# A hybrid pooling/SSM/MoE block on one core: second half of the down matrices behind experts three and four, last round by tiles, u read back ahead of the output projection

## The chip, the cores and the metric

The kernel runs on one core of a Trainium2 chip. The metric is the device time of one execution in microseconds. The profile is one more execution, taken by the hardware profiler; its times below count from the first instruction.

## The reference

One layer over 256 latent tokens of width 1024, with a prefix of 256 context tokens, float32 throughout:

```python
mod = silu(c) @ w_mod + b_mod              # shift, scale and gate, twice
h   = rmsnorm(x, g_mix) * (1 + sc1) + sh1  # the same for the context
u   = h @ w_in                             # 512 columns pooled, 512 for the SSM
pool = pool_mixer(u[:, :512])              # centred means, four windows
ssm  = glu(gelu(scan_fwd(u_ssm) + scan_bwd(u_ssm) + d * u_ssm))
x   = x + g1 * (concat(pool, ssm) @ w_out)
h2  = rmsnorm(x, g_ffn) * (1 + sc2) + sh2
eidx, gate = route(h2)                     # best of 4 groups, top 2 of its 8 experts
y   = moe(h2)                              # 32 experts: (silu(x@Wg) * (x@Wu)) @ Wd, hidden width 512
out = rmsnorm(x + g2 * y, g_final)
```

The scans start from the final state of the context's scan.

## The kernel before

Each engine has a program of its own and the engines meet at semaphores (`wait_ge`, `then_inc`). SP issues nearly all loads, in one hand-written order: its queue is in order, so a wait in SP's program holds back every load behind it. ScalarE and GpSimd issue a few transfers of their own.

**The mixer.** The modulation's first two thirds are products on TensorE, of `w_mod` in eight row chunks each (`mod_chunk`, semaphore `mod_used`). The last third is loaded in eight pieces of 1 MiB (`last_third(j, gate)`, four with gate 0 for the scale, four with gate 1 for the gate) and summed on VectorE by `mod_sum` (lines 1405 and 1408, semaphore `mod2_used`). GpSimd's `mod_bias` adds the bias row to each, and `modulation(gate)` on TensorE sums over the partitions.

For the SSM, u is computed in four parts (`u_ssm`), taken from PSUM by ScalarE into `ut`, written to the DRAM tensor `u_scratch` in two halves (line 1041, `u_out0`, `u_out1`) and read back in another layout by eight reads each (line 308, `u8_in0`, `u8_in1`). `state_inputs(h)` on TensorE (line 655) makes the inputs of the scans from each half, ScalarE takes them out (`take_states`), and VectorE runs the scan of each half, then fills `HP` (`hp_ready`). Before the second half's reads SP issues `wo_ssm`, the lower half of `w_out`, 2 MiB. Behind ScalarE's `take_states(0)` stand two copies of the lag kernels (`KT`), which TensorE waits for, and 15 transfers that build a Toeplitz table (`toeplitz`, `toep_in`), which both TensorE and the writing of `HP` wait for.

Then come GELU (ScalarE), the GLU product (line 759), VectorE's products into `cat` (`cat_ssm`, line 1204), the product with `w_out` (`mix_pool`, line 711, for the pooled half and line 799 for the SSM half), the residual, the second norm, and the router. `modulation(1)` (line 748) stands ahead of the counting product (`counts`, lines 823 and 824), and the one-hot gather (line 835) takes rows of each expert's tokens into `xm`.

**The experts.** They go by in rounds of four, `four(i)`, i from 0 to 7. `wts` has two buffers for the gate and up matrices of one expert each (4 MiB), and there are four places for down matrices (2 MiB each). A round moves 24 loads of 1 MiB: 8 for experts one and two, 8 for three and four, 8 for the down matrices. SP's functions for them are `next_two(i - 1)` (experts one and two of round i), `second_two(i)` (experts three and four) and `downs(i, half)` (half of each down matrix). `second_two(i)` waits for `gu_half`, which TensorE raises after each half of an expert; each of its four waits stands in front of two loads. `downs(i, 0)` waits until round i - 1 has used its first halves (`down_half`), `downs(i, 1)` until that round's `down` has ended (`down_mm`). In the last round the second halves go as two quarters each (`down_load_one`).

TensorE's round is: `gate_up(i, 0)` to `gate_up(i, 3)` (lines 863 and 864), transposes of the hidden rows (line 879), the scatter of the round before (line 841), `down(i)` (line 903, 128 instructions) and the gathers for the next round (line 835). A matmul of a float32 operand appears as two instructions.

**The end.** In the last round `down` goes over n = 2h + t (column half h, token tile t) in the order 0, 1, 2, 3. VectorE scales each n by the gate (`four_out`). TensorE scatters both tiles' first column halves, then both second ones. ScalarE squares and sums each tile, GpSimd makes (mean + eps) ** -0.5 of the sum, VectorE multiplies each half tile by that and by `g_final` in one instruction (line 1589), and SP and ScalarE store.

SP's order in the inner rounds and in the last one is:

```python
with sp.Fori(1, last_four) as i:
    downs(i, 0)
    downs(i, 1)
    second_two(i)
    next_two(i)
downs(last_four, 0)
second_two(last_four)
```

Of the kernel before, what the change touches and what calls it, by code (L numbers as in the profile page):

```python
# [7 lines left out]
ALU = mybir.AluOpType  # L8
# [50 lines left out]
def hybrid_block(nc, x, ctx, w_mod, columns, ssm_bc, b_mod_rows, w_in, w_out, w_pool, w_glu, w_router, b_router,  # L59
# [9 lines left out]
    FC = F // P  # L69
    NC = T // L  # L70
    DG = 32
    GP = 16

    with ExitStack() as stack:
# [183 lines left out]

        def store(eng, t, h):

            eng.dma_start(out[0, t * P:(t + 1) * P, 512 * h:512 * (h + 1)],
                          xn2[:, t, 512 * h:512 * (h + 1)]).then_inc(S("out_done"), 16)

        @block.sync
        def _(sp):
# [36 lines left out]
            for h in range(2):  # L302
                if h == 1:
                    sp.wait_ge(S("u_ssm_mm"), 4)
                    sp.dma_start(wo_ssm, w_out_v[:, 4:8, :]).then_inc(S("wo_ssm_in"), 16)
                sp.wait_ge(S(f"u_out{h}"), 16)
                for s in range(L):
                    sp.dma_start(ra[SG * s:SG * (s + 1), 0:2048].rearrange("i (g n) -> i g n", g=8)[:, :, 128 * h:128 * h + 128],
                                 u_dram.rearrange("(g i) (w s n) -> w s i g n", g=8, w=2, s=L)[h, s]).then_inc(S(f"u8_in{h}"), 16)
# [6 lines left out]

            sp.wait_ge(S("mod_used"), 14)
# [88 lines left out]
        def _(gp):  # L406
            gp.memset(cb[:, 2048:4096], 0.0).then_inc(S("cb_zero"), 1)

            gp.wait_ge(S("mhalf_set"), 1)
# [64 lines left out]
            def mod_bias(gate):  # L474

                gp.wait_ge(S("mod2_used"), KD * gate + KD)
                for n in range(2):
                    j = 2 * gate + n
# [8 lines left out]
            for t in range(2 * NT):  # L487
                if t == NT:

                    gp.dma_start(gfb, g_final.rearrange("(a d) -> a d", a=1).broadcast_to([P, D])).then_inc(S("gf_in"), 16)  # L490
                gp.wait_ge(S("ss2_ready" if t < NT else "ss3_ready"), t % NT + 1)
# [3 lines left out]
                if t == NT - 1:  # L495
# [4 lines left out]
                    gp.memset(PT, 0.0).then_inc(S("zeroed"), 1)  # L500

        @block.tensor
        def _(pe):
# [238 lines left out]
            def modulation(gate):  # L743

                pe.wait_ge(S("mod2_sum"), 2 * gate + 2)
                for h in range(2):
                    j = 2 * gate + h
                    mm = pe.matmul(ps[:, 6 + h, :], ones, acc[:, 512 * j:512 * j + 512], start=True, stop=True)
                return mm

            modulation(0).then_inc(S("scale_mm"), 1)
# [66 lines left out]
            modulation(1).then_inc(S("gate_mm"), 1)  # L818
# [8 lines left out]
            BANKS = (6, 7, 4, 5)  # L827
            GATHER = (6, 7, 5, 6)
# [9 lines left out]
            def scatter(h, stop=False):  # L838

                for t in range(NT):  # L840
                    mm = pe.matmul(ps[:, 2 * t + h, :], PT[:, t, :], oS[:, 2 * h + t, :], start=False, stop=stop, skip_group_check=True)  # L841
                return mm
# [47 lines left out]
            def down(i, last):  # L890

                pe.wait_ge(S("hid_ready"), 4 * i + 4)
                for f in range(FC):
# [4 lines left out]
                    for n in range(4):  # L898
# [739 lines left out]
```

## Time and profile before

| | |
|---|---|
| median of 3 runs | 661.68 us (659.23 to 661.77) |
| the profiled execution | 661.11 us |
| its span, first to last instruction | 659.3 us |
| mean granted clock of TensorE | 0.965 |
| TensorE busy | 588.4 us (89%) |
| VectorE busy | 196.1 us (30%) |
| ScalarE busy | 132.0 us (20%) |
| moved by DMA | 249.02 MB, mean 378 GB/s |

### The profile page before, as it was taken

What the parts mean: (1) busy time and instruction counts of PE and PEld (TensorE: products, weight loads), DVE (VectorE), ACT (ScalarE), POOL (GpSimd) and SP (SyncE); (2) the same over time, 40 slices, a digit from 0 to 9 for tenths busy, and PEclk for the clock granted to TensorE, in tenths of its full rate; (3) what the DMA queues carried; (4) which work ended last, traced back from release to release, by engine and by line L of the source; (5) the groups of instructions that cost most, each with busy time, mean ns of one, the idle gap of its engine ahead of it and who ended that gap; (6) DMA issues with size and microseconds to landing.
All of it is one profiled execution on the core that took longest, in us unless ns stands there. A gap on an engine that the chain in (4) does not pass through costs nothing.

```text
span 659.3 us, 9355 instructions
## 1 busy us (share of the span) xinstructions
PE 588.4 (89%) x3770; PEld 249.9 (38%) x3770; DVE 196.1 (30%) x426; ACT 132.0 (20%) x226; POOL 53.3 (8%) x103
## 2 busy tenths in 40 slices
PE   1999968889899997899799879979997997899995
PEld 0454544455553342234233323423342342234331
DVE  7998458988730020002001000200100010002003
ACT  8661312031213111012020201111021102012111
POOL 3894000012010000000000000000000000000000
PEclk9999979999979999999799989989998999999999
DMA  8993999998779999999999999999999999999951
GB/s 330 418 402 110 319 327 292 401 410 351 299 281 409 422 419 421 422 417 422 422 421 420 423 421 421 420 421 422 422 422 422 423 421 421 421 421 375 403 227 64
DMA packets 43609, 249.02 MB, mean 378 GB/s; under 512 B 4776, under 2 KB 7480, under 8 KB 17216
## 3 DMA queue, kind: packets, MB, share of 16 engines
q1 hardware_dynamic: 41240, 243.93, 91.2%
q10 hardware_dynamic: 1992, 3.68, 1.7%
q0 software_dynamic: 352, 1.07, 0.5%
q8 instruction: 17, 0.28, 0.2%
q14 instruction: 8, 0.07, 0.0%
HBM read 244.46 MB, written 2.11 MB: 374 GB/s over the span
## 4 chain that ended last, share of the span: by engine, by line
PE 56%; DMA 21%; DVE 2%; issue 1%; SPq 0%; ACT 0%; POOL 0%; DVEq 0%
PE ps L863 21%; DMA wts<-in_w_up 21%; PE ps L903 17%; PE ps L835 5%; PE ps L841 5%; PE ps L799 2%; PE ps L711 1%; PE ps L879 1%; PE ps L759 1%; PE ps L727 1%; SPq L243 0%; PE ps L864 0%; DVE rc L1204 0%; DVE ra L1589 0%; PE ps L791 0%
## 5 line engine op out<-in xcount | busy, mean ns | idle before, releaser
L863 PE MATMUL ps<-wts,ra 128*64 128x512 f32 x512 | 242.5, 626 | 34.2 <-DMA wts<-in_w_up 33.0
L864 PE MATMUL ps<-wts,ra 128*64 128x512 f32 x512 | 242.6, 626 | 0.0
L863 PEld LDWEIGHTS ps<-wts,ra 128*64 128x64 f32 x512 | 70.0, 143 | 180.3 <-issue 133.5
L903 PE MATMUL ps<-wts,ra 128*32 128x512 f32 x512 | 111.4, 593 | 0.0
L903 PE MATMUL ps<-rc,ra 128*32 128x512 f32 x512 | 111.4, 593 | 0.0
L1204 DVE TENSOR_TENSOR ra<-ra,ps 128x256 f32<-128x256 f32 x32 | 13.5, 422 | 268.7 <-ACT ra L1150 268.6
L1144 ACT COPY ra<-ps 128x512 f32<-128x512 f32 x32 | 33.6, 1050 | 218.6 <-PE ps L864 218.6
L864 PEld LDWEIGHTS ps<-wts,ra 128*64 128x64 f32 x512 | 70.0, 143 | 0.0
L903 PEld LDWEIGHTS ps<-wts,ra 128*32 128x32 f32 x512 | 29.1, 110 | 73.2 <-issue 73.2
L1204 DVE TENSOR_TENSOR cb<-ps,ra 128x512 f32<-128x512 f32 x32 | 22.1, 692 | 103.4 <-PE ps L903 103.4
L1139 ACT COPY ra<-ps 128x512 f32<-128x512 f32 x32 | 18.8, 586 | 148.4 <-PE ps L835 148.4
L492 POOL TENSOR_SCALAR small<-small 128x1 f32<-128x1 f32 x4 | 0.8, 188 | 475.6 <-ACT ra L1185 467.7
L835 PEld LDWEIGHTS ps<-cb,ra 128*128 128x128 f32 x256 | 31.4, 200 | 13.6 <-issue 8.6
L835 PE MATMUL ps<-cb,ra 128*128 128x128 f32 x256 | 34.5, 291 | 1.1 <-issue 1.1
L841 PE MATMUL ps<-cb 128*128 128x512 f32 x68 | 32.9, 606 | 0.0
L622 PE MATMUL ps<-ra,wts 128*128 128x512 f32 x64 | 29.6, 600 | 0.6 <-ACT ra L1025 0.6
L903 PEld LDWEIGHTS ps<-rc,ra 128*32 128x32 f32 x512 | 29.2, 110 | 0.0
L1204 DVE TENSOR_TENSOR cb<-cst,ut 128x256 f32<-128x256 f32 x16 | 6.7, 421 | 47.9 <-PE ps L835 46.6
L879 PEld LDWEIGHTS ps<-cst,ra 128*128 128x128 f32 x128 | 14.2, 141 | 17.2 <-issue 15.3
L520 PE MATMUL ps<-wts,sil 128*32 128x512 f32 x96 | 13.4, 649 | 7.4 <-DMA wts<-in_w_mod 7.2
L879 PE MATMUL ps<-cst,ra 128*128 128x128 f32 x128 | 18.8, 280 | 0.0
L841 PEld LDWEIGHTS ps<-cb 128*128 128x128 f32 x68 | 11.6, 190 | 15.5 <-issue 14.6
(226 smaller groups left out, 509.4 us busy)
## 6 DMA issues: line engine op xcount, KB each, us to landing
wts<-in_w_up SPq DMA_DIRECT2D x64, 1024.0 KB, 15.5
wts<-in_w_gate SPq DMA_DIRECT2D x64, 1024.0 KB, 13.4
wts<-in_w_down SPq DMA_DIRECT2D x30, 1024.0 KB, 8.6
rc<-in_w_down SPq DMA_DIRECT2D x30, 1024.0 KB, 12.4
wts<-in_w_mod SPq DMA_DIRECT2D x16, 1024.0 KB, 13.4
r<-in_w_mod SPq DMA_DIRECT2D x6, 1024.0 KB, 10.9
wts<-in_w_out SPq DMA_DIRECT2D x2, 2048.0 KB, 11.5
wts<-in_w_in SPq DMA_DIRECT2D x2, 1024.0 KB, 19.8
```

The costliest lines, as they stand in the source:

```text
L520: mm = pe.matmul(ps[32 * j:32 * j + 32, bank, :], silc[:, k, :], w[:, 512 * j:512 * j + 512], start=False, stop=(k == KD - 1))
L622: mm = pe.matmul(ps[:, 4 + q % 2, :], WBs[:, k, P * q:P * q + P], hT[:, k, :], start=(k == 0), stop=(k == KD - 1))
L799: mm = pe.matmul(ps[:, n, :], cat[:, 4 + k, P * (n // 2):P * (n // 2) + P], wo_ssm[:, k, 512 * (n % 2):512 * (n % 2) + 512], start=False, ...
L835: mm = pe.matmul(o, h2P[:, t, k, :], Pm[:, t], start=True, stop=True, skip_group_check=True)
L841: mm = pe.matmul(ps[:, 2 * t + h, :], PT[:, t, :], oS[:, 2 * h + t, :], start=False, stop=stop, skip_group_check=True)
L863: pe.matmul(ps[0:64, 4 + b, :], st, Wg[b][:, k, :], start=(k == 0), stop=(k == KD - 1))
L864: mm = pe.matmul(ps[64:128, 4 + b, :], st, Wu[b][:, k, :], start=(k == 0), stop=(k == KD - 1))
L879: mm = pe.transpose(ps[:, 6 + j % 2, P * f:P * f + P], gu[:, j % 2, P * f:P * f + P], ident)
L903: mm = pe.matmul(ps[32 * j:32 * j + 32, BANKS[n], :], hid[:, j, f, SLOTS * t:SLOTS * t + SLOTS], Wd[j][:, f, 512 * h:512 * h + 512], start ...
L1139: act.copy(xm[:, 2 * r:2 * r + 2], ps[:, GATHER[r], :].rearrange("p (k e s) -> p k e s", k=2, e=4)).then_inc(S("xm_ready"), 1)
L1144: act.copy(gu[:, j % 2, :].rearrange("p (f q) -> p q f", f=FC), ps[:, 4 + j % 2, :].rearrange("p (q f) -> p q f", f=FC)).then_inc(S("gu_co ...
L1204: return dve.tensor_tensor(o, a, b, op)
```

## The change

- **u.** The eight reads of the second half go out as soon as its write has landed, four from SP and four from ScalarE (behind `take_states(0)`), and the load of `wo_ssm` moves behind them and behind modulation chunks 6 and 7.
- **The gate's bias.** GpSimd adds the bias row only for the scale. For the gate, TensorE adds it in `gate_product`, with a product of one row for each half.
- **The order of the expert loads.** Round one is written out in the old order. From round two on `second_two(i)` stands between the two halves of `downs`. In the last round `second_two` comes ahead of `downs(last_four, 0)`.
- **The last round.** n goes 0, 2, 1, 3, so both halves of tile 0 come first. VectorE multiplies by sqrt(D) and `g_final` without waiting for the norm's factor, and the factor (of the sum, not the mean) is applied afterwards in place, to three half tiles on ScalarE and one on VectorE. The stores are spread anew.
- Two pairs of semaphores become one each (`consts_set`, and `ss2_ready` for `ss3_ready`).

```diff
+        def u8_load(eng, h, lags):
+            for s in lags:
+                eng.dma_start(ra[SG * s:SG * (s + 1), 0:2048]..., u_dram...[h, s]).then_inc(S(f"u8_in{h}"), 16)
...
             for h in range(2):
-                if h == 1:
-                    sp.wait_ge(S("u_ssm_mm"), 4)
-                    sp.dma_start(wo_ssm, w_out_v[:, 4:8, :]).then_inc(S("wo_ssm_in"), 16)
                 sp.wait_ge(S(f"u_out{h}"), 16)
-                for s in range(L):
-                    sp.dma_start(ra[SG * s:SG * (s + 1), 0:2048]..., u_dram...[h, s]).then_inc(S(f"u8_in{h}"), 16)
+                u8_load(sp, h, range(L // 2 if h else L))
                 for k in range(3 + 3 * h, min(6 + 3 * h, KD)):
                     mod_chunk(1, k)
...
+            sp.wait_ge(S("u_ssm_mm"), 4)
+            sp.dma_start(wo_ssm, w_out_v[:, 4:8, :]).then_inc(S("wo_ssm_in"), 16)
             sp.wait_ge(S("mod_used"), 14)
...
             second_two(0)
             next_two(0)
+            downs(1, 0)
+            downs(1, 1)
+            second_two(1)
+            next_two(1)
...
-            with sp.Fori(1, last_four) as i:
+            with sp.Fori(2, last_four) as i:
                 downs(i, 0)
+                second_two(i)
                 downs(i, 1)
-                second_two(i)
                 next_two(i)
+            second_two(last_four)
             downs(last_four, 0)
-            second_two(last_four)
...
-            for t in range(NT):
-                sp.wait_ge(S("fin_ready"), 2 * t + 1)
-                store(sp, t, 0)
+            for h in range(2):
+                sp.wait_ge(S("fin_act"), h + 1)
+                store(sp, 0, h)
+            sp.wait_ge(S("fin_ready"), 1)
+            store(sp, 1, 1)
...
# GpSimd
-            mod_bias(0)
-            mod_bias(1)
+            mod_bias()
+            gp.wait_ge(S("mod2_used"), 2 * KD)
...
+            for t in range(NT):
+                gp.wait_ge(S("ss2_ready"), NT + t + 1)
+                gp.tensor_scalar(ms2[:, 2 + t:3 + t], ms2[:, 2 + t:3 + t], float(D * EPS), None, ALU.add)...
+                gp.tensor_tensor(rstd2[:, 2 + t:3 + t], ms2[:, 2 + t:3 + t], mhalf, ALU.pow)...
...
# TensorE
+            def gate_product():
+                pe.wait_ge(S("mod2_used"), 2 * KD)
+                for h in range(2):
+                    j = 2 + h
+                    pe.matmul(ps[:, 6 + h, :], ones[32 * j:32 * j + 1, :], modrow[32 * j:32 * j + 1, 2, :], start=True, stop=False)
+                    mm = pe.matmul(ps[:, 6 + h, :], ones, acc[:, 512 * j:512 * j + 512], start=False, stop=True)
...
-            modulation(1).then_inc(S("gate_mm"), 1)
+            gate_product().then_inc(S("gate_mm"), 1)
...
+            TILE_ORDER = (0, 2, 1, 3)
...
-                    for n in range(4):
+                    for n in (TILE_ORDER if last else range(4)):
...
-            pe.wait_ge(S("out_copy"), 4 * last_four + 6)
             pe.wait_ge(S("pt_copy"), last_four + 2)
-            scatter(0, True)
-            pe.wait_ge(S("out_copy"), 4 * last_four + 8)
-            for t in range(NT):
-                pe.matmul(ps[:, 2 * t + 1, :], PT[:, t, :], oS[:, 2 + t, :], start=False, stop=True,
+            for at, n in enumerate(TILE_ORDER):
+                h, t = n // 2, n % 2
+                pe.wait_ge(S("out_copy"), 4 * last_four + 5 + at)
+                pe.matmul(ps[:, 2 * t + h, :], PT[:, t, :], oS[:, n, :], start=False, stop=True,
                           skip_group_check=True).then_inc(S("y_ready"), 1)
...
# ScalarE
             take_states(0)
+            act.wait_ge(S("u_out1"), 16)
+            u8_load(act, 1, range(L // 2, L))
...
-                act.wait_ge(S("y_ready"), t + 1)
+                act.wait_ge(S("y_ready"), 2 * t + 2)
...
+            for at, (t, h) in enumerate(((0, 0), (0, 1), (1, 0))):
+                act.wait_ge(S("rstd2_ready"), NT + t + 1)
+                act.wait_ge(S("gf_scaled"), at + 1)
+                v = xn2[:, t, 512 * h:512 * h + 512]
+                act.mul(v, v, rstd2[:, 2 + t:3 + t]).then_inc(S("fin_act"), 1)
+            act.wait_ge(S("fin_act"), 3)
+            store(act, 1, 0)
...
# VectorE
-            four_out(last_four)
+            four_out(last_four, (0, 2, 1, 3))
...
             for t in range(NT):
-                dve.wait_ge(S("rstd2_ready"), 3 + t)
+                dve.wait_ge(S("ss2_ready"), NT + t + 1)
                 for h in range(2):
                     c0 = slice(512 * h, 512 * h + 512)
-                    dve.scalar_tensor_tensor(xn2[:, t, c0], ps[:, 2 * t + h, :], rstd2[:, 2 + t:3 + t], gfb[:, c0],
-                                             ALU.mult, ALU.mult).then_inc(S("fin_ready"), 1)
+                    dve.scalar_tensor_tensor(xn2[:, t, c0], ps[:, 2 * t + h, :], ROOT_D, gfb[:, c0],
+                                             ALU.mult, ALU.mult).then_inc(S("gf_scaled"), 1)
+            dve.wait_ge(S("rstd2_ready"), 2 * NT)
+            dve.wait_ge(S("gf_scaled"), 2 * NT)
+            v = xn2[:, 1, 512:1024]
+            dve.tensor_scalar(v, v, rstd2[:, 3:4], None, ALU.mult).then_inc(S("fin_ready"), 1)
```

## Rows read from the trace of the kernel before

**Rows 1.** Stretches by round, six and seven; columns as in the first line.

```profile
core 0: us, PE busy (x) PEld busy (x) DVE busy (x) ACT busy (x) POOL busy (x), PEclk, DMA share, GB/s
537.23:596.85 59.62, 53.70 (x316) 20.36 (x315) 5.54 (x11) 8.10 (x13) 0.00 (x0) 0.97 1.01 422
596.85:649.07 52.22, 52.03 (x316) 19.91 (x315) 5.21 (x10) 8.14 (x13) 0.00 (x0) 1.00 0.73 289
```

**Rows 2.** The chain that ended last, rounds six and seven: start, us, what.

```profile
574.60 0.64 PE ps L863
...
596.85 1.98 PE ps L835 x16
...
626.82 0.64 PE ps L863
...
635.20 13.87 PE ps L903 x128
```

**Rows 3.** Timeline around the bounce of u; the last line is line 1041's landings.

```profile
76.44 0.33 ACTq L1041 DMA_DIRECT2D u_scratch<-ut  x1
...
85.52 3.89 SPq L308 DMA_DIRECT2D ra<-u_scratch  x8
...
92.29 6.67 PE L655 MATMUL ps<-ra,wts 128*64 128x64 f32 x128 [5.32 <-DMA ra<-u_scratch]
...
DMA to landing us min/median/max: 3.3/6.2/9.1
```

**Rows 4.** Timeline of VectorE, the start of the second scan.

```profile
100.14 1.36 DVE L1204 TENSOR_TENSOR cb<-wts,cb 128x256 f32<-128x256 f32 x3 [7.43 <-ACT wts L1054]
```

**Rows 5.** Stretches of the mixer, columns as in rows 1.

```profile
76.00:104.00 28.00, 22.68 (x316) 14.82 (x312) 15.22 (x50) 9.42 (x16) 0.00 (x0) 0.88 0.85 296
104.00:152.00 48.00, 41.37 (x440) 24.73 (x435) 42.78 (x102) 10.88 (x20) 2.51 (x2) 1.00 1.02 385
```

**Rows 6.** The gate's first third: issue, landing; its use, cat_ssm, w_out's product (timeline, chain).

```profile
131.25 0.38 SPq L295 DMA_DIRECT2D wts<-in_w_mod  x1
...
wts<-in_w_mod SPq DMA_DIRECT2D x1, 1024.0 KB, 10.2
...
143.63 0.75 DVE L1405 TENSOR_SCALAR cb<-wts,sil 128x1024 f32<-128x1024 f32 x1
...
151.18 2.03 DVE L1204 TENSOR_TENSOR wts<-rc 128x256 f32<-128x256 f32 x4
...
153.21 3.43 PE ps L799 x8
```

**Rows 7.** Timeline of TensorE from the counts to the first gate_up.

```profile
179.93 0.41 PE L823 MATMUL ps<-cb,cst 128*128 128x64 f32 x2 [1.89 <-DVE cb L1204]
...
181.80 3.75 PE L835 MATMUL ps<-cb,ra 128*128 128x128 f32 x16 [1.07 <-issue]
...
187.53 1.06 PE L863 MATMUL ps<-wts,ra 128*64 128x512 f32 x1
...
188.38 1.06 PE L863 MATMUL ps<-wts,ra 128*64 128x512 f32 x1
```

**Rows 8.** Stretches chosen for the granted clock (PEclk), columns as in rows 1.

```profile
92.20:98.40 6.20, 6.11 (x116) 6.11 (x118) 0.45 (x3) 2.73 (x4) 0.00 (x0) 0.51 1.00 412
...
115.40:118.80 3.40, 1.97 (x8) 1.44 (x8) 2.90 (x15) 1.31 (x4) 0.00 (x0) 1.00 1.03 349
...
176.00:180.00 4.00, 2.11 (x6) 0.67 (x4) 3.52 (x17) 1.01 (x1) 0.00 (x0) 1.00 1.01 420
180.00:184.00 4.00, 2.92 (x14) 2.77 (x15) 3.59 (x16) 0.12 (x1) 0.91 (x1) 0.53 1.01 422
```

**Rows 9.** Round seven: SP's first load for expert three, and a stretch behind it.

```profile
602.46 0.33 SPq L243 DMA_DIRECT2D wts<-in_w_gate  x1
...
602.00:604.00 2.00, 2.00 (x16) 1.65 (x15) 0.00 (x0) 0.46 (x1) 0.00 (x0) 1.00 0.63 197
```

**Rows 10.** Timeline of the end: ScalarE's square, VectorE's four products, GpSimd's power.

```profile
653.09 1.02 ACT L1185 ACTIVATE ra<-ps 128x1024 f32<-128x1024 f32 x1
...
654.03 2.73 DVE L1589 SCALAR_TENSOR_TENSOR ra<-ps,small,r 128x512 f32<-128x512 f32 x4 [4.20 <-POOL small L494]
...
654.57 0.55 POOL L494 TENSOR_TENSOR small<-small 128x1 f32<-128x1 f32 x1
```

More of the change, by code:

```diff
@@ L69, in hybrid_block @@
     FC = F // P
+    ROOT_D = float(math.isqrt(D))
     NC = T // L
+    assert ROOT_D * ROOT_D == D
     DG = 32
@@ L473, in _, with mod_bias @@
             gp.dma_start(ctmp, w_router.rearrange("(p k) e -> p k e", k=KD)).then_inc(S("wr2_in"), 16)
[L474 to L478, printed above, removed]
+            def mod_bias():
+                gp.wait_ge(S("mod2_used"), KD)
+                for j in range(2):
                     a = acc[32 * j:32 * j + 1, 512 * j:512 * j + 512]
@@ L483, in _ @@
             gp.wait_ge(S("bmod_in"), 16)
-            mod_bias(0)
-            mod_bias(1)
+            mod_bias()
+            gp.wait_ge(S("mod2_used"), 2 * KD)
             gp.dma_start(brb, b_router.rearrange("(a d) -> a d", a=1).broadcast_to([P, NE])).then_inc(S("br_in"), 16)
[L487 to L491, printed above, removed]
+            for t in range(NT):
+                gp.wait_ge(S("ss2_ready"), t + 1)
                 gp.tensor_scalar(ms2[:, t:t + 1], ms2[:, t:t + 1], 1.0 / D, EPS, ALU.mult, ALU.add).then_inc(S("ms2_ready"), 1)
@@ L500, in _ @@
                     gp.memset(PT, 0.0).then_inc(S("zeroed"), 1)
+            gp.dma_start(gfb, g_final.rearrange("(a d) -> a d", a=1).broadcast_to([P, D])).then_inc(S("gf_in"), 16)
+            for t in range(NT):
+                gp.wait_ge(S("ss2_ready"), NT + t + 1)
+                gp.tensor_scalar(ms2[:, 2 + t:3 + t], ms2[:, 2 + t:3 + t], float(D * EPS), None, ALU.add).then_inc(S("ms2_ready"), 1)
+                gp.wait_ge(S("ms2_ready"), NT + t + 1)
+                gp.tensor_tensor(rstd2[:, 2 + t:3 + t], ms2[:, 2 + t:3 + t], mhalf, ALU.pow).then_inc(S("rstd2_ready"), 1)
         @block.tensor
@@ L741, in _, with scale_product @@
             mix_pool(3, (1,))
-            def modulation(gate):
-                pe.wait_ge(S("mod2_sum"), 2 * gate + 2)
+            def scale_product():
+                pe.wait_ge(S("mod2_sum"), 2)
                 for h in range(2):
-                    j = 2 * gate + h
-                    mm = pe.matmul(ps[:, 6 + h, :], ones, acc[:, 512 * j:512 * j + 512], start=True, stop=True)
-                return mm
-            modulation(0).then_inc(S("scale_mm"), 1)
+                    mm = pe.matmul(ps[:, 6 + h, :], ones, acc[:, 512 * h:512 * h + 512], start=True, stop=True)
+                return mm
+            def gate_product():
[4 more added lines that the diff above has]
+                    mm = pe.matmul(ps[:, 6 + h, :], ones, acc[:, 512 * j:512 * j + 512], start=False, stop=True)
+                return mm
+            scale_product().then_inc(S("scale_mm"), 1)
             pe.wait_ge(S("wglu_in"), 16)
@@ L836, in gather, with scatter @@
                 mm.then_inc(S("gather_mm"), 1)
-            def scatter(h, stop=False):
+            def scatter(h):
                 for t in range(NT):
-                    mm = pe.matmul(ps[:, 2 * t + h, :], PT[:, t, :], oS[:, 2 * h + t, :], start=False, stop=stop, skip_group_check=True)
-                return mm
+                    pe.matmul(ps[:, 2 * t + h, :], PT[:, t, :], oS[:, 2 * h + t, :], start=False, stop=False, skip_group_check=True)
             pe.wait_ge(S("g2_ready"), 1)
@@ L1564, in four_hidden, with four_out @@
                        ALU.mult).then_inc(S("hid_ready"), 1)
-            def four_out(i):
-                for n in range(4):
-                    dve.wait_ge(S("down_mm"), 4 * i + n + 1)
+            def four_out(i, order=range(4)):
+                for at, n in enumerate(order):
+                    dve.wait_ge(S("down_mm"), 4 * i + at + 1)
                     tt(oS[:, n, :], ps[:, BANKS[n], :], g2b[:, 512 * (n // 2):512 * (n // 2) + 512], ALU.mult).then_inc(S("out_copy"), 1)
```

20 lines of the change are left out of this document (9 added, 11 removed).

## The prediction

> **What bounds the kernel now.** I read the stretches by round first. An inner round of the experts (`four(i)`) takes 59.6 us in which the 16 DMA engines are busy throughout at 422 GB/s; it moves 24 loads of 1 MiB, so one load costs 59.6/24 = 2.48 us. TensorE is busy 53.7 us of it. The last round is the other way round: 52.2 us, TensorE busy 52.0 [rows 1]. So rounds one to six are set by the stream of weights, and the last by TensorE. The chain of waits gives the marks inside a round [rows 2]: the last piece of expert four lands, TensorE starts on it at 574.60, and round seven starts 22.25 us later (596.85). In round seven the same piece comes 29.97 us after the round's start (626.82), `down` begins at +38.35 and ends at +52.2 (635.20 + 13.87).
>
> Ahead of the experts I read the timeline from 60 to 190 us, for what each engine waits. The mixer's u goes to memory and back (`u_scratch`). For its second half the write was issued at 76.44, just behind SP's 2 MiB load of `wo_ssm`, and took 9.1 us where the first half's took 3.3; the reads went out from 85.52, and TensorE stood 5.32 us before `state_inputs(1)` at 92.29 [rows 3]. VectorE, done with its first scan, stood 7.43 us before the second at 100.14, which leads to `hp_ready` [rows 4]. That looks like 7.4 us to win, but the stretches by DMA say something else: from 104 to 152 us the DMA engines are never idle [rows 5].
>
> **The change, part by part. 1: u ahead of the output projection.** With `wo_ssm` behind the reads, the write takes the 3.3 us of an empty queue and ends at 79.8. SP then issues four reads and ScalarE four (3.9 us for eight on SP [rows 3], so about 2 us on each), and they land 2 to 3 us later, near 85 to 87. Behind ScalarE's four stand the two copies of `KT`, which TensorE wants at 83.3: about 1 us late, TensorE gets to `state_inputs(1)` near 88 instead of 92.3. The Trainium skill (DMA: Bandwidth & Descriptors, "Issuing engines are not separate DMA queues") says that issuing from two engines saves only the issue time, since the transfers share the same engines. By that the split itself is worth under 2 us and the reorder all the rest; no row contradicts it, and the sum stays as it is.
>
> `state_inputs(1)` ran at half clock after its wait (0.51 from 92.2 to 98.4 [rows 8]); without the wait it should end near 92, so the second scan follows the first at once, and `hp_ready` comes 7.4 us earlier.
>
> Now who is late next. The DMA engines were idle 15% of the 28 us from 76 to 104, some 4.2 us, and not at all after that [rows 5]. After the change the hole around the bounce (76.4 to about 83.5, in which only 1 MiB of u moves) is some 4.3 us idle, and from then on all loads stand in the queue. The same bytes, the same idle time: the stream is where it was. The first third of the gate's modulation (`last_third(0, 1)`), issued at 131.25, landed after 10.2 us, at 141.45 [rows 6]. VectorE reached its use at 143.63; moved 7.4 us forward it would want it at 136.2 and so stands about 5.3 us. From that use to the first product of `cat_ssm` VectorE took 151.18 - 143.63 = 7.55 us [rows 6], so that starts at 141.5 + 7.55 = 149.05, 2.1 us earlier, and the first is done at 149.6. TensorE has finished `mix_pool` at 153.21 - 7.4 = 145.8 and waits 3.8 us; its product with `wo_ssm` starts at 149.6, 3.6 us earlier. After its 5.3 us wait at 92.2 the clock stood at half for 6.2 us [rows 8], 3.1 us lost; I take 2.2 here, for a shorter wait (between nothing and 3.1). Part 1 gives 3.6 - 2.2 = **1.4 us**, bounds 0 and 7.4.
>
> **2: the gate's bias on TensorE.** GpSimd no longer adds it; TensorE makes two products of 512 columns more, 0.86 us each (3.43 us for four [rows 6]), 1.7 us in all. They lie in its 1.89 us of idleness before `counts` at 179.93 [rows 7]. The copy of `g2b` ends about 0.7 us before the gather would need it. Uncovered it would cost 1.7 us. But it fills a hole. Of 176 to 180 TensorE was busy 2.11 us and the clock then fell to 0.53; of 115.4 to 118.8 it was busy 1.97 of 3.4 and the clock stayed at 1.00 [rows 8]. With 3.8 of 4 us busy I expect the clock to stay. Then the 16 matmuls of the first gather take 2.0 instead of 3.75 us [rows 7], and the first four passes behind them, which came 0.85 us apart [rows 7] where a pass takes 0.43 (3.43/8), gain 1.7: **3.5 us**, bounds 0 (it falls anyway) and 3.5. Nothing hides it, because the loads of round zero's experts three and four wait for those very passes.
>
> **3: half the down matrices behind experts three and four.** G is a pair's eight loads (19.9 us), D a half of the down matrices (four loads, 9.93 us). The stream was next G, D, D, second G; it becomes next G, D, second G, D. In round two the stream has delivered its first D at start - 22.25 + 19.86 + 9.93 = start + 7.5. SP issues the second G only when TensorE has used half an expert, at start + 5.6 (602.46 in round seven [rows 9]), so the queue runs nearly dry. Round seven of the kernel before has just this order already: its second G landed at +29.97, where the stream alone gives 7.5 + 19.9 = 27.4, and the rows show 197 GB/s at 602 to 604 [rows 9]. So 2.5 us are lost and 9.93 won: round two's second G lands 7.4 us earlier, at +29.97, which TensorE can follow, as it did in round seven, and round three starts 7.4 us earlier. In rounds three to six the D that was put off lies before the next G, so the first D lands at +17.5, 12 us after SP's first wait is over: never dry, 59.6 us each as before. Round seven: the next G lands at +7.5, the second G (2.5 us lost again) at +29.9, D at +39.9. `down` is ready at +38.35 and now waits 1.5 us; the two quarters behind it land at +44.9 and +49.8, wanted at +46.8 and +50.3. `down` ends at +53.7 instead of +52.2. Part 3: 7.4 - 1.5 = **5.9 us**, bounds 0 and 7.4.
>
> **4: the last round by tiles.** E is the end of `down` (649.07). Tile 0 is complete after two scatters instead of three, 0.86 us earlier. The second square then starts at its own tile's end, E + 3.7, instead of 653.09 = E + 4.0, and ends with its read at E + 4.85 [rows 10]. VectorE, which had waited for GpSimd's power, now multiplies by `gfb` as soon as a square is through: four times 0.66 us (2.73 for four [rows 10]), the last ending at E + 6.2. GpSimd's power for tile 1 ends at E + 5.8. The last scaling of 512 columns costs 0.4 on VectorE (0.75 for 1024 [rows 6]) and 0.55 on ScalarE (1.02 for 1024 [rows 10]): E + 6.75 on both, where it was 654.03 + 2.73 = E + 7.7. **1.0 us**, bounds 0 and 1.5. The renamed semaphores and ROOT_D cost nothing.
>
> The sum is 1.4 + 3.5 + 5.9 + 1.0 = 11.8 us. The profiled execution took 661.11 us (its span of 659.3 and 1.8 around it), so 649.3; the median of the runs is 0.6 above it: 649.9, say **650**.
>
> **Rivals.** (a) The clock falls at the gather all the same. For it: two other waits of about 1 us follow. 650 + 3.5 = 653.5. The skill's page TensorE: Matmul & The Clock Gate ("HAM oscillation") says that waits between groups of matmuls bring the half clock back; by that rule it is this case, though 115.4 to 118.8 speaks against. (b) The modulation's third is not late, because the stream is denser than I reckon: 1.4 becomes 7.4, 644. Against it: the 104 to 152 row. (c) ScalarE's reads of u share the engines with the modulation chunks that SP sends at 82 and land after 92: part 1 gives nothing or costs 1, and with parts 2 or 3 smaller the time is 651 to 657. (d) The change of order does nothing, because rounds three to six also lose 2.5 us each: 10 us back, 660, no change. (e) Slower, the same place: SP's first wait in `second_two` now has only one D queued behind it. If that D landed at the round's start and not at +17.5, each of rounds three to six would lose up to 5.6 + 2 = 7.6 us, 30 in all: 680. It decides from 11.8/4 = 3.0 us a round on. Against it stands the order of the stream, which puts D and G, 29.8 us, in front of it.
>
> **Numbers.** Forecast 0.42, (a) 0.25, (b) 0.12, (c) 0.11, (d) 0.06, (e) 0.04. The range from 644 to 656.5 holds (a), (b), the forecast and most of (c). A change within 0.5% (3.3 us) is about what this measurement can't tell from none. Faster: 0.91 (forecast, a, b, c and a little of d), same 0.05, slower 0.04.
>
> **What would show it.** TensorE's wait at `state_inputs(1)` under 1 us; VectorE waiting 4 to 6 us for a `w_mod` load near 136 to 141; TensorE waiting 3 to 4 us before `wo_ssm`'s product; granted clock 1.00 at the first gather; round two 52 us, three to six 59.6, seven 53.7 with a wait for a down matrix in front of `down`; from the end of `down` to the end of the span 9.2 instead of 10.2. The prediction is wrong if a middle round is longer than 60, or if `hp_ready` does not move.

## The result and the profile after

The changed kernel took **653.07 us** in the median of five runs (652.09 to 656.37) where the kernel before took 661.48: ratio 0.988, 95% interval 0.986 to 0.991. Forecast: 650, range 644 to 656.5. Time and range held; most of the terms behind them did not. The experiments say that two were too small, two too large, and that the gains of two parts do not add up.

The profiled execution was the slowest of the five (656.37, span 654.2), so I ran the changed kernel again unchanged (`e9_again`: 653.68 us, ratio 0.991, 0.988 to 0.993). Its profiled execution took 652.21 us, span 650.1. Where the two differ I show both. One run below, 656.42 us in `e6_banks`, was a slow one and is left out of that kernel's median and ratio.

First the mixer, first profile after, timeline of TensorE (start, us, engine, line, op, tiles, shapes, count, [idle before <- what ended it]). Lines 655, 799, 770, 748, 835 and 863 of before are now 669, 821, 792, 769/770, 858 and 885.

```profile
87.50 3.95 PE L669 MATMUL ps<-ra,wts 128*64 128x64 f32 x128
...
148.81 5.37 PE L821 MATMUL ps<-wts 128*128 128x512 f32 x8 [2.28 <-DVE wts L1231]
...
170.23 5.30 PE L792 MATMUL ps<-rc,cst 128*128 128x512 f32 x8
175.46 1.12 PE L769 MATMUL ps<-mr,cst 1*128 1x512 f32 x2
...
181.03 2.02 PE L858 MATMUL ps<-cb,ra 128*128 128x128 f32 x16 [0.89 <-ACT ra L1156]
185.84 0.61 PE L885 MATMUL ps<-wts,ra 128*64 128x512 f32 x1 [2.79 <-DVEq L1575]
```

`state_inputs(1)` starts at 87.50 without a wait (92.29 after 5.32 us before [rows 3]). The SSM product of `w_out` starts at 148.81 instead of 153.05, behind a new wait of 2.28 us for VectorE. (The chain of before starts it at 153.21 [rows 6], its timeline at 153.05:)

```profile
153.05 3.60 PE L799 MATMUL ps<-wts 128*128 128x512 f32 x8
```

The first gather takes 2.02 us instead of 3.75 [rows 7]. Yet it starts at 181.03, only 0.77 us earlier, and the first gate product at 185.84, only 0.81 us earlier than the 186.65 of the kernel before. What stands in front of it is now named: a release by VectorE, 2.79 us (the row names line 1575, a register load of VectorE's; the release itself is the `sem_inc` of `out_copy` behind it). Of 4.2 us won at 149, 2.4 are left at `start_outputs` (170.23 for 172.64) and 0.8 at 186.

VectorE, the same profile (timeline):

```profile
93.35 1.36 DVE L1231 TENSOR_TENSOR cb<-wts,cb 128x256 f32<-128x256 f32 x3
...
135.36 1.66 DVE L1446 SCALAR_TENSOR_TENSOR rc<-ut,vt,ps 128x256 f32<-128x256 f32 x4 [2.75 <-PE ps L753]
140.53 0.75 DVE L1432 TENSOR_SCALAR cb<-wts,sil 128x1024 f32<-128x1024 f32 x1 [3.52 <-DMA wts<-in_w_mod]
```

The second scan follows the first at once (93.35; 100.14 before [rows 4]), and at 140.53 VectorE has waited 3.52 us for the gate's first third, the wait that takes the place of the one removed.

Stretches of the first profile after: rounds two, three, six and seven, then chosen ones (columns as in rows 1).

```profile
297.10:350.75 53.65, 52.09 (x318) 20.10 (x315) 5.55 (x11) 8.10 (x13) 0.00 (x0) 1.00 0.99 406
350.75:410.44 59.69, 54.54 (x318) 20.43 (x314) 5.55 (x11) 8.11 (x13) 0.00 (x0) 0.94 1.01 421
529.81:589.48 59.67, 53.85 (x319) 20.45 (x315) 5.55 (x11) 8.08 (x13) 0.00 (x0) 0.97 1.01 422
589.48:644.19 54.71, 52.09 (x319) 20.73 (x315) 5.21 (x10) 8.13 (x13) 0.00 (x0) 1.00 0.85 339
...
594.00:598.00 4.00, 4.00 (x28) 2.41 (x26) 0.00 (x0) 1.17 (x2) 0.00 (x0) 1.00 0.44 119
149.00:153.00 4.00, 4.00 (x6) 1.61 (x6) 3.79 (x6) 0.00 (x0) 0.00 (x0) 0.58 1.01 421
171.00:173.00 2.00, 2.00 (x4) 0.74 (x3) 1.88 (x12) 0.10 (x1) 0.00 (x0) 0.50 1.02 422
...
187.00:190.00 3.00, 3.00 (x10) 1.18 (x8) 0.00 (x0) 0.00 (x0) 0.00 (x0) 0.53 0.87 359
```

And the second profile of the same kernel, rounds two, three and seven:

```profile
296.24:348.04 51.80, 51.80 (x318) 19.97 (x314) 5.55 (x11) 8.13 (x13) 0.00 (x0) 1.00 0.98 403
348.04:407.04 59.00, 54.78 (x319) 20.54 (x315) 5.55 (x11) 8.12 (x13) 0.00 (x0) 0.94 1.01 422
586.02:640.06 54.04, 52.10 (x319) 20.60 (x315) 5.21 (x10) 8.13 (x13) 0.00 (x0) 1.00 0.90 362
```

Round two is the round the change shortens: 53.65 us in one execution, 51.80 in the other, in which TensorE never stands still; the middle rounds stay at the stream's 59.7. Round seven has a dry stretch in both, in which little is left in the queue to move (119 GB/s from 594 to 598 here). The half clock stands in three places of the first profile: at 149 to 153, behind the new wait; around 171, under `start_outputs` (line 792); and at 187 to 190, under the first gate products. In the kernel before it was at 92 to 98 and at 180 to 184 [rows 8].

The chain of waits of the first profile, before and under the last `down`:

```profile
610.41 19.77 DMA rc<-in_w_down
630.32 13.94 PE ps L925 x128
```

`down` begins 40.8 us into the round (630.32 - 589.48); the timeline gives its wait as 1.67 us. The end of it (timeline, the first profile):

```profile
648.94 1.94 ACT L1214 ACTIVATE ra<-ra,small 128x512 f32<-128x512 f32 x3
649.67 1.65 SPq L270 DMA_DIRECT2D out_x<-ra  x3
650.48 0.49 DVE L1621 TENSOR_SCALAR ra<-ra,small 128x512 f32<-128x512 f32 x1
650.90 0.40 ACTq L270 DMA_DIRECT2D out_x<-ra  x1
```

and from the same stretch the view of the DMA issues (KB each, us from issue to landing):

```profile
out_x<-ra SPq DMA_DIRECT2D x3, 256.0 KB, 2.2
out_x<-ra ACTq DMA_DIRECT2D x1, 256.0 KB, 2.6
```

`down` ends at 644.26 (630.32 + 13.94). The last scaling ends 6.7 us after it (650.97 - 644.26; 7.7 before), but the span ends 9.9 us after it, against 10.2.

### The profile page after: what moved, and what is told of

It reads as the page before. It is cut to its first block, busy times and chain, and to the rows that moved or that the text cites. A ratio compares the mean times of both kernels' runs of the same rounds, so it can differ in the third digit from the quotient of the medians.

```text
span 654.2 us, 9323 instructions
## 1 busy us (share of the span) xinstructions
PE 589.0 (90%) x3774; PEld 248.9 (38%) x3774; DVE 196.4 (30%) x427; ACT 133.6 (20%) x229; POOL 51.6 (8%) x101
## 3 DMA queue, kind: packets, MB, share of 16 engines
q10 hardware_dynamic: 2424, 3.68, 1.7%
q0 software_dynamic: 352, 1.07, 0.5%
## 4 chain that ended last, share of the span: by engine, by line
PE 54%; DMA 22%; DVE 2%; issue 1%; SPq 1%; ACT 0%; DVEq 0%; ACTq 0%
PE ps L885 23%; PE ps L925 17%; DMA wts<-in_w_up 16%; PE ps L858 5%; PE ps L864 4%; DMA rc<-in_w_down 3%; DMA wts<-in_w_mod 2%; PE ps L821 2%; PE ps L901 1%; PE ps L792 1%; SPq L246 1%; PE ps L886 0%; DVE cb L1435 0%; DVE ra L1616 0%; PE ps L770 0%
## 5 line engine op out<-in xcount | busy, mean ns | idle before, releaser
L858 PEld LDWEIGHTS ps<-cb,ra 128*128 128x128 f32 x256 | 29.8, 191 | 13.7 <-issue 7.6
L858 PE MATMUL ps<-cb,ra 128*128 128x128 f32 x256 | 32.8, 281 | 0.9 <-ACT ra L1156 0.9
L864 PE MATMUL ps<-cb 128*128 128x512 f32 x64 | 30.9, 606 | 0.0
L821 PE MATMUL ps<-wts 128*128 128x512 f32 x32 | 16.1, 656 | 2.3 <-DVE wts L1231 2.3
```

Source lines behind the costliest of these rows:

```text
L821: mm = pe.matmul(ps[:, n, :], cat[:, 4 + k, P * (n // 2):P * (n // 2) + P], wo_ssm[:, k, 512 * (n % 2):512 * (n % 2) + 512], start=False, ...
L858: mm = pe.matmul(o, h2P[:, t, k, :], Pm[:, t], start=True, stop=True, skip_group_check=True)
```

## The experiments

Medians are of 5 to 12 runs each; ratios are to the kernel before on the same chip (its medians 660.7 to 661.4). No kernel leaves work out.

| run | what | median us | ratio (95%) |
|---|---|---|---|
| `e1_order` | before, part 3 alone | 653.80 | 0.988 (0.987 to 0.990) |
| `e2_u` | before, part 1 alone | 657.61 | 0.994 (0.992 to 0.995) |
| `e3_bias` | before, part 2 alone | 660.83 | 1.000 (0.998 to 1.002) |
| `e4_tail` | before, part 4 alone | 660.94 | 1.000 (0.998 to 1.001) |
| `e10_u_order` | before, parts 1 and 3 | 653.20 | 0.988 (0.986 to 0.991) |
| `e9_again` | all four parts | 653.68 | 0.991 (0.988 to 0.993) |
| `e11_sp_reads` | all four, eight reads on SP | 654.44 | 0.990 (0.988 to 0.993) |
| `e5_thirds` | all four + gate's thirds first | 650.25 | 0.985 (0.983 to 0.988) |
| `e6_banks` | all four + banks released early | 651.12 | 0.984 (0.980 to 0.988) |
| `e7_last` | all four + one down load ahead | 651.07 | 0.986 (0.983 to 0.989) |
| `e8_all` | all four + the last three | **644.70** | 0.977 (0.975 to 0.979) |
| `e12_all_oldbias` | `e8_all` without part 2 | 644.56 | 0.976 (0.974 to 0.979) |

**The order alone.**

```diff
-                downs(i, 1)
                 second_two(i)
+                downs(i, 1)
                 next_two(i)
...
-            downs(last_four, 0)
             second_two(last_four)
+            downs(last_four, 0)
```

> The kernel before with the new order of SP's expert loads alone. As predicted (round two's last gate piece 7.4 us earlier, down in round seven 1.5 us late): 5.9 us faster, ratio 0.991. Theory from the trace after (5.9 won in round two, 0.35 lost at the start of the chain of round three, 2.4 lost before the last down): 3.2 us faster, ratio 0.995, with the last round at 54.6 us and a wait of about 1.7 us for a down matrix ahead of down. Rival, the two losses are made by the other parts: 5.9 or more.

7.6 us, more than the forecast's 5.9 and more than twice the 3.2 I had read off the first profile after. That reading fell: round two took 51.8 us here and in nine of the ten profiles with this order; the 53.65 was one execution's. The last round took 54.0 with a wait of 1.67 us before `down`. From the first `down` of round one to the last, the first instructions lie 343.8 us apart (283.77 to 627.59) where it was 350.2 before (284.93 to 635.13): 6.4 us by the profiles. The other 1.1 us between these two profiles lies ahead of the first `down` (223.79 for 224.84), where this edit changes nothing.

**u alone.** The diff's `u8_load`, and:

```diff
-                if h == 1:
-                    sp.wait_ge(S("u_ssm_mm"), 4)
-                    sp.dma_start(wo_ssm, w_out_v[:, 4:8, :])...
                 sp.wait_ge(S(f"u_out{h}"), 16)
...
+            sp.wait_ge(S("u_ssm_mm"), 4)
+            sp.dma_start(wo_ssm, w_out_v[:, 4:8, :])...
```

> The kernel before with the reads of u ahead of the output projection alone (four of the second half's eight on ScalarE). As predicted: 1.4 us faster (ratio 0.998), with the 5.3 us wait before state_inputs(1) gone and a new wait of 3 to 5 us of VectorE for the gate's modulation. Theory from the trace after: SSM product 2.5 us earlier, all of it carried to the experts, 2.5 us (0.996). Rival, the stream is denser with the reads early and the third lands earlier: 4 to 7 us.

3.8 us. The timeline of TensorE:

```profile
148.45 3.67 PE L802 MATMUL ps<-wts 128*128 128x512 f32 x8 [2.41 <-DVE wts L1209]
...
177.27 2.73 PE L838 MATMUL ps<-cb,ra 128*128 128x128 f32 x16 [1.24 <-issue]
```

The same wait stands before the SSM product (2.41 us), but here the clock did not fall behind it: 3.67 us for its first eight, where the changed kernel took 5.37. The gather starts at 177.27, 3.7 us before that of `e4_tail` (180.96), which has the mixer of the kernel before.

**The bias alone.**

```diff
+            def gate_product():
+                pe.wait_ge(S("mod2_used"), 2 * KD)
+                for h in range(2):
+                    ... pe.matmul(ps[:, 6 + h, :], ones[...], modrow[...], start=True, stop=False)
+                    ... pe.matmul(ps[:, 6 + h, :], ones, acc[...], start=False, stop=True)
```

> The kernel before with the gate's bias added by TensorE alone. As predicted: full clock at the first gather, 3.5 us faster (0.995). Theory from the trace after: the gather takes 2 us instead of 3.75, but the first gate product waits for VectorE's release of the banks that the router used, at the same time as before; 0 to 1 us faster (1.000 to 0.9985). Rival, the clock falls at the gather all the same: 0, with the gather at 3.75 us.

Nothing that can be told (by the ratio 0.1 us, give or take 1.1). Timeline of TensorE from `start_outputs` on, first with the bias on TensorE:

```profile
171.60 5.38 PE L777 MATMUL ps<-rc,cst 128*128 128x512 f32 x8
...
182.47 2.02 PE L842 MATMUL ps<-cb,ra 128*128 128x128 f32 x16 [0.89 <-ACT ra L1140]
187.29 0.61 PE L870 MATMUL ps<-wts,ra 128*64 128x512 f32 x1 [2.80 <-DVEq L1555]
```

and without it (`e4_tail`):

```profile
171.81 5.38 PE L784 MATMUL ps<-rc,cst 128*128 128x512 f32 x8
177.02 1.88 PE L762 MATMUL ps<-cb,cst 128*128 128x512 f32 x4
179.09 0.41 PE L837 MATMUL ps<-cb,cst 128*128 128x64 f32 x2 [0.19 <-DVE cb L1221]
180.96 2.02 PE L850 MATMUL ps<-cb,ra 128*128 128x128 f32 x16 [1.24 <-issue]
185.82 1.00 PE L877 MATMUL ps<-wts,ra 128*64 128x512 f32 x1 [2.83 <-DVEq L1565]
```

From `start_outputs` to the gather: 10.87 us with, 9.15 without, so the two extra products stand on the path with all their 1.7 us. The hole of 1.89 us in which I had put them is 0.19 us here, since `start_outputs` ran at half clock (5.38 us; 3.68 at full). And the old kernel's gather also ran at full clock (2.02 us) in this execution. The gather's duration does not matter anyway: the first gate product starts 4.86 us after the gather's start here, and 4.85 in the kernel before, whose gather took 3.75 (186.65 - 181.80 [rows 7]). What it follows is VectorE's last instruction ahead of the release, a memset; `before`, then the changed kernel (timelines of VectorE):

```profile
185.58 0.07 DVE L1546 MEMSET ut<- 128x8 f32 x1
```

```profile
184.78 0.07 DVE L1573 MEMSET ut<- 128x8 f32 x1
```

The first gate product starts 1.07 us after it in the one (186.65) and 1.06 in the other (185.84), and 1.06 to 1.10 in all eleven profiles with the release in its old place. What does come back is the clock under the first gate products, by the stretches, `e4_tail` and then the changed kernel again:

```profile
186.00:190.00 4.00, 4.00 (x12) 1.41 (x11) 0.43 (x1) 0.00 (x0) 0.00 (x0) 0.58 0.85 346
```

```profile
186.00:190.00 4.00, 3.81 (x18) 1.49 (x19) 0.43 (x1) 0.00 (x0) 0.00 (x0) 1.00 0.91 347
```

Without the bias on TensorE the clock fell under the gather or the first gate products in all six profiles; with it in two of eight, the first profile of the changed kernel among them. First gate product to first `down` took 37.7 us in `e4_tail` (223.55 - 185.82) and 36.2 in `e3_bias` (223.45 - 187.29): 1.5 back for 1.7 paid.

**The last round alone.**

```diff
-                    dve.scalar_tensor_tensor(xn2[...], ps[...], rstd2[...], gfb[...], ALU.mult, ALU.mult)
+                    dve.scalar_tensor_tensor(xn2[...], ps[...], ROOT_D, gfb[...], ALU.mult, ALU.mult)
...
+                act.mul(v, v, rstd2[:, 2 + t:3 + t]).then_inc(S("fin_act"), 1)
```

> The kernel before with the last round by tiles and the norm's factor applied afterwards, alone. As predicted: 1.0 us faster (0.9985). Theory from the trace after: the last scaling ends 0.9 us earlier after the end of down, but the stores that follow take 2.5 instead of 2.1 us to land, so 0.2 to 0.5 us. Rival, the stores' landing varies by run and is no part of the change: 0.9 us in the median. Together with the other three parts the sum should be 8.4 us if the parts add up; if it comes out far from that, they do not.

0.4 us by the medians and 0.1 by the ratio, within the noise (give or take 1.1). Its last store landed after 2.7 us, so the longer landing belongs to the change and not to the run: the last two stores of 256 KB, which were issued about 0.66 us apart, now go out together when both scalings end. That it is their sharing of the DMA engines fits (256 KB at 422 GB/s is 0.6 us), but no run moves one store alone.

**Three further edits on the changed kernel.**

```diff
# e5_thirds
-            sp.wait_ge(S("hp_ready"), 1)
-            for half in range(2):
-                down_load(sp, lambda j: j, half, (1,))
             ... last_third(j, 1), j from 0 to 3 ...
+            for half in range(2):
+                down_load(sp, lambda j: j, half, (1,))
# e6_banks: VectorE
             link(dve.tensor_reduce(best[:, 0:1], ps[:, 5, 2 * NE:4 * NE], AX.X, ALU.max))
+            dve.sem_inc(S("out_copy"), 4)
...
-            dve.sem_inc(S("out_copy"), 4)
# e7_last
+            sp.wait_ge(S("down_half"), last_four)
+            down_load(sp, lambda j: (4 * last_four + j) % NE, 0, (0,))
             second_two(last_four)
-            downs(last_four, 0)
+            down_load(sp, lambda j: (4 * last_four + j) % NE, 0, (1, 2, 3))
```

> The changed kernel with both halves of expert one's down matrix (2 MiB) loaded behind the four pieces of the gate's modulation instead of ahead of them. Theory: the pieces land 5 us earlier, so VectorE's 3.5 us wait for w_mod and TensorE's 2.3 us wait before the SSM product of w_out vanish, and the clock does not fall there: 3.5 to 5 us faster than the changed kernel, 12 to 13 us faster than the kernel before (ratio 0.981). Rival, something else holds the SSM product (GELU, the GLU product or the bytes of the first experts): 0 to 1 us against the changed kernel (ratio 0.987).

> The changed kernel with VectorE's release of the router's PSUM banks put right behind its last read of them instead of behind the copies of positions and gates. Theory: the first gate product starts at about 183 instead of 185.8 us, 2 to 2.7 us faster than the changed kernel (ratio to the kernel before 0.984). Rival, the loads for experts one and two bound round zero: the start moves and round one doesn't, 0 us (0.9885).

> The changed kernel with one of the last round's four first-half loads of the down matrices put ahead of the loads for experts three and four, the other three behind them. Theory: this fills the dry stretch at the start of the round (119 GB/s from 594 to 598 us), expert four lands no later and the last down starts without its wait of 1.7 us: 1.5 to 2.4 us faster than the changed kernel (ratio 0.985 to the kernel before). Rival, the load that goes ahead pushes expert four by 2.5 us: 0 us, with the wait moved to a gate product.

> The changed kernel with all three of those edits. If they add up: 7 to 9 us faster than the changed kernel, about 645 us, ratio 0.975. If the first two serve the same wait at the router or the stream of round zero bounds: 4 to 5 us (0.981).

With the thirds first VectorE goes from one to the next without a wait, and so does TensorE; timelines of VectorE and of TensorE in `e5_thirds`:

```profile
135.21 1.66 DVE L1445 SCALAR_TENSOR_TENSOR rc<-ut,vt,ps 128x256 f32<-128x256 f32 x4 [2.65 <-PE ps L752]
136.78 0.75 DVE L1431 TENSOR_SCALAR cb<-wts,sil 128x1024 f32<-128x1024 f32 x1
```

```profile
144.49 1.88 PE L724 MATMUL ps<-wts 128*128 128x512 f32 x4
146.20 3.60 PE L820 MATMUL ps<-wts 128*128 128x512 f32 x8
```

The product starts 2.6 us earlier and at full clock, and `start_outputs` too runs at full clock (3.68 us). So the place of those 2 MiB made the new wait: SP issued the first piece at the same time in both (124.30 in the changed kernel, 124.23 here), but it landed after 16.2 us there and after 11.3 here. SP's wait for `hp_ready`, which the edit drops as well, held nothing back. The time against the changed kernel's 653.07 and 653.68 is about 3 us lower, just below the 3.5 to 5 expected. The profiled execution was this kernel's fastest (646.27 for a median of 650.25), so its rows show more than the edit gives on average. With the banks released early the first gate product follows the gather (timeline of TensorE, `e6_banks`):

```profile
181.45 2.02 PE L858 MATMUL ps<-cb,ra 128*128 128x128 f32 x16 [0.89 <-ACT ra L1156]
183.41 0.64 PE L885 MATMUL ps<-wts,ra 128*64 128x512 f32 x1
...
212.71 0.64 PE L885 MATMUL ps<-wts,ra 128*64 128x512 f32 x1 [1.22 <-DMA wts<-in_w_up]
```

1.96 us after its start instead of 4.8 to 4.9: the release was the bound there. A new wait for the stream of round zero (1.22 us at 212.71) takes part of the 2.9 back; the medians fell by 2.0 to 2.6 us (3.0 to 4.4 by the ratios). With one down load ahead, the last `down` has no wait, the round takes 52.84 us where it took 54.0 to 54.7, and its dry stretch is gone (stretches of `e7_last`):

```profile
584.85:637.69 52.84, 52.03 (x319) 19.92 (x315) 5.20 (x10) 8.13 (x13) 0.00 (x0) 1.00 0.89 368
589.00:593.00 4.00, 4.00 (x28) 2.47 (x26) 0.00 (x0) 1.08 (x2) 0.00 (x0) 1.00 1.02 426
```

The three add up within the noise (6.8 to 8.6 us by the single medians, 8.4 to 9.0 together): 644.70 us, 2.3% below the kernel before; with `e12_all_oldbias`, equal to it, the fastest version.

**The parts together, and who reads u.** `e9_again` has no edit; `e10_u_order` has the two diffs of `e1_order` and `e2_u`; `e11_sp_reads`:

```diff
-                u8_load(sp, h, range(L // 2 if h else L))
+                u8_load(sp, h, range(L))
...
-            act.wait_ge(S("u_out1"), 16)
-            u8_load(act, 1, range(L // 2, L))
```

> The changed kernel once more, unchanged. The parts measured singly add up to 11.9 us (7.6 + 3.8 + 0.1 + 0.4), the whole gave 8.4 in five runs, and its profiled execution was the slowest of them: 654.2 us of span, with round two at 53.65 us where five of the kernels with the new order show 51.8. Theory, that was an execution of the slow end and the parts add up: median 649.5 to 651.5, ratio 0.983 to 0.985, round two at 51.8. Rival, the parts stand in each other's way: 652 to 654, ratio 0.987 to 0.990.

> The kernel before with two parts, the reads of u ahead of the output projection and the order of the expert loads. Theory, the parts add up: 11.4 us faster, ratio 0.983, and equal to the changed kernel within a microsecond, since the gate's bias and the last round by tiles are worth nothing that shows. Rival, the two together give less than their sum, because round one's stream starts earlier and meets the dry stretch of round two otherwise: 8 us, ratio 0.988. Second rival, the bias on TensorE costs something when u comes early: this one is faster than the changed kernel by 2 us or more.

> The changed kernel with all eight reads of the second half of u issued by SP, none by ScalarE. Theory (the split saves only issue time, 2 of 3.9 us, and the second scan waits for the first scan, not for the reads): state_inputs(1) starts up to 2 us later, near 89, the second scan starts when the first is through, and the time is the same within 1 us. Rival, the later reads or the modulation chunks 6 and 7 behind them are on the path: 1 to 2 us slower than the changed kernel.

The theory that the parts add up fell: the product of the single ratios is 0.982 (649.4 us); the two large parts alone give 0.988, and all four 0.988 and 0.991. For the two large parts the product would be 0.982, 3.9 us from what they gave, with an uncertainty of 2.3. u, worth 3.8 us by itself, adds 0.6 to the order by the medians (653.80 to 653.20, on different chips) and 0.2 by the ratios, give or take 2. One part of that can be seen (timeline of TensorE, `e10_u_order`):

```profile
148.00 5.37 PE L806 MATMUL ps<-wts 128*128 128x512 f32 x8 [2.24 <-DVE wts L1213]
```

The half clock behind the wait, missing in `e2_u`, is here (1.7 us more for the first eight); it came in five of seven profiles of kernels with the wait. The gather then starts at 178.51, 1.24 us later than in `e2_u`. That leaves about 2 us of u's gain unaccounted for in the medians (below).

With SP reading alone the issue of all eight took 4.49 us from 79.54, `state_inputs(1)` started at 87.67 (87.50 with the split) after a wait of 0.45 us, and the median lies 0.8 to 1.4 us above the changed kernel's two, within the noise: ratio 0.990. So the split brings nothing that shows. By the Trainium skill (DMA: Bandwidth & Descriptors, "Issuing engines are not separate DMA queues") it could save issue time alone, and the trace agrees: the start of `state_inputs(1)` moved by 0.17 us.

**The bias, once more.** `e8_all` with GpSimd adding the bias for the gate again (`mod_bias(1)`), and:

```diff
-            gate_product().then_inc(S("gate_mm"), 1)
+            modulation(1).then_inc(S("gate_mm"), 1)
```

> The kernel with the three further edits (modulation thirds first, early release of the banks, one down load ahead), with the gate's bias given back to GpSimd. Theory: TensorE's two extra products lie on the path, so the first gather starts 1.7 us earlier without them (9.15 instead of 10.87 us after the start of start_outputs, as in the other kernels), but the clock falls once more by the first gate products or the loads of round zero bound it, so the last down moves by 0 to 1 us and the time is the same as with the bias on TensorE (ratio 0.976 to 0.979). Rival one, the extra products cost their full 1.7 us: ratio 0.974. Rival two, they hold the clock up over the router and are worth it: 1.5 us slower or more, ratio 0.979 or above.

The time is as expected, the reason only half. Timeline of TensorE, `e12_all_oldbias` (bias on GpSimd):

```profile
165.90 3.68 PE L786 MATMUL ps<-rc,cst 128*128 128x512 f32 x8
...
173.19 0.41 PE L839 MATMUL ps<-cb,cst 128*128 128x64 f32 x2 [1.90 <-DVE cb L1225]
175.06 3.58 PE L852 MATMUL ps<-cb,ra 128*128 128x128 f32 x16 [1.24 <-issue]
178.57 0.64 PE L879 MATMUL ps<-wts,ra 128*64 128x512 f32 x1
```

and `e8_all` (bias on TensorE):

```profile
165.66 3.68 PE L793 MATMUL ps<-rc,cst 128*128 128x512 f32 x8
174.84 2.02 PE L859 MATMUL ps<-cb,ra 128*128 128x128 f32 x16 [0.89 <-ACT ra L1157]
176.79 0.65 PE L886 MATMUL ps<-wts,ra 128*64 128x512 f32 x1
```

Here `start_outputs` runs at full clock, and the picture is the predicted one to the tenth: both gathers start 9.2 us after it, so the extra products are hidden; the hole of 1.90 us is there without them, and the clock falls behind it (3.58 us); with them it stays (2.02). The first gate product then starts 1.8 us earlier, and round zero gives it back: its first `down` comes at 214.27 instead of 214.64, because `e8_all` waits 1.22 us for a load at 206.0.

## Why the prediction was right or wrong

The second profile of the changed kernel lies 9.2 us below that of before by its span (650.1 for 659.3). By stretches: up to the first gate product 0.5 (186.65 to 186.19); from there to the first `down` (224.84 and 222.26) 2.1 (38.2 to 36.1 us); rounds two and three 8.4; the last round -1.8; the tail 0.3; the other rounds -0.2. The forecast's sum was 11.8. The four parts measured singly add up to 11.9 (3.8, 0.1, 7.6 and 0.4), yet the whole gave 8.4 and 7.1 by the medians. That the two sums agree is luck, and the time lay inside the range because the range left room for part 2 to give nothing.

- **The bound.** Right: rounds three to six stay at 59.0 to 59.7 us and 421 GB/s, round seven at TensorE's 52 plus what it waits.
- **Part 1, 1.4 us.** The mechanism was right step by step: no wait at `state_inputs(1)`, the second scan at once, a new wait of 3.5 us (predicted 5.3) for `last_third(0, 1)`, one of 2.3 (3.8) on TensorE. The mis-sized term is "I take 2.2 here" for the half clock. It measured 1.7 when it came (5.37 - 3.67) and nothing in `e2_u`, which gave 3.8 us; the gather came 3.7 us earlier without it and 2.45 with it, both against `e4_tail`. The bound "between nothing and 3.1" held it. Rival (b), 7.4 us, fell, since the third was late; rival (c) fell too, since the reads had landed when `state_inputs(1)` started at 87.50, well before 92.
- **Part 2, 3.5 us.** This is the step that failed, and the largest miss. "They lie in its 1.89 us of idleness before `counts`" took one execution's hole for the kernel's: the hole exists only while `start_outputs` runs at full clock, and it ran at half in ten of the fourteen profiles. And "Nothing hides it": VectorE's release of the banks hid the gather's length, a wait that the row of before lists as `issue` (1.10 us). The row of `e2_u` does the same for 2.18 us, and why the profile names VectorE in some executions and not in others stays open. Part 2 is worth 0.1 us, give or take 1.1.
- **Rival (a)**, the clock falls at the gather all the same, did not happen: 2.02 us in all eight profiles with the bias on TensorE. Three of six without it have 2.02 too. Waits between groups of matmuls do bring the half clock back here, as the Trainium skill says of waits for a DMA (TensorE: Matmul & The Clock Gate, "HAM oscillation"): behind the wait of 2.1 to 3.3 us for VectorE before the SSM product it came in five of seven profiles. But it stood at other places than the gather, at 149, at 171 and under the first gate products, by execution. The time near rival (a)'s 653.5 is no proof of it.
- **Part 3, 5.9 us.** Right in kind, 6.4 by the profiles of `e1_order` (7.6 by the medians), made of 8.4 won in rounds two and three and 1.8 lost in the last. Round two took 51.8 (52.2 forecast), round three 59.0 (59.6), round seven 54.0 (53.7) with the wait for a down matrix of 1.67 (1.5). Rivals (d) and (e) fell: no middle round is longer than 59.7.
- **Part 4, 1.0 us.** The last scaling ended at E + 6.71 (E is the end of `down`), as worked out (6.75), but the step "from the end of `down` to the end of the span 9.2" failed: 9.9. From the end of the last scaling to the end of the span it took 2.5 us before and 3.2 now; the last two stores start together and the last lands 0.5 us later. I had carried the old landing of 2.1 us along unchanged. 0.3 us remained.
- **The sum.** That terms of different stages add was not argued, only done. Against order alone, u brings 0.6 us in the median, where by the profiles it brings 2.6. **This stays open**: the profiles of `e1_order` and `e10_u_order` differ by 2.6 us at the first `down` (223.79 and 221.17) and keep it to the end, but the latter's profiled execution was 1.5 us faster than its median, and the executions without a profile show no stretches.

## What to carry to other kernels

A hole seen in one profiled execution may be there only while the work ahead of it runs at full clock: before filling it, check that it is there when that work runs at half clock as well. Where the idle time of a row says `issue`, look for a release by another engine just before the row starts; shortening the row may uncover it, and moving the release is then the cheap edit (2 lines, about 2 us here). And when a load is moved so that one engine is ready earlier, ask which load it wants next and put that one first: with it, the release and one load moved into a dry stretch the gain was 16 us, where the change alone gave 7 to 8.

## What was not expected of the hardware

TensorE's clock falls at different places in executions of the same code: the mixer of the kernel before showed a gather of 3.75 us (`before`) and of 2.02 us (`e1_order`, `e4_tail`), and `start_outputs` of 3.68, 5.38 and 6.34 us. Differences of 1 to 2 us in the mixer between two profiles are therefore no evidence for an edit, and the runs of one kernel lay up to 7.8 us apart (645.87 to 653.71 in `e6_banks`). Round two of the changed kernel, by its code the same everywhere, took 53.65 us in one profile and 51.8 in nine, with loads landing about 2 us later after the same issue times; why is open.
